# Stationary tiles 576 bytes apart instead of 512 in a two-layer diffusion backbone step

## The reference

```python
def _swiglu(t, wg, wu, wd):
    return (jax.nn.silu(t @ wg) * (t @ wu)) @ wd

def _moe(t, router, wg, wu, wd):
    logits = (t @ router).astype(F32)
    top_v, top_i = lax.top_k(logits, TOP_K)
    gates = jax.nn.softmax(top_v, axis=-1)
    combine = jnp.sum(jax.nn.one_hot(top_i, N_EXPERTS, dtype=F32) * gates[..., None], axis=1)
    out = jnp.zeros_like(t)
    for e in range(N_EXPERTS):
        out = out + combine[:, e:e + 1].astype(t.dtype) * _swiglu(t, wg[e], wu[e], wd[e])
    return out
```

## Time and profile before

| | us |
|---|---|
| median of 3 runs | 1528.2 |
| lowest and highest | 1527.68, 1528.72 |
| the profiled execution | 1526.36 |
| its span, first to last instruction | 1524.5 |

### The profile page before, as it was taken

One profiled execution on the slowest core, in us unless ns is written; L12 is line 12 of the kernel. 1 busy time (PEld: TensorE's weight loads), 2 busy tenths in 40 slices (PEclk: granted clock), 3 DMA queues, 4 the chain that ended last, 5 costly groups with the idle time before them and its releaser, 6 DMA issues.

```text
span 1524.5 us, 21865 instructions
## 1 busy us (share of the span) xinstructions
PE 1471.9 (97%) x7705; PEld 1216.1 (80%) x7705; DVE 1153.6 (76%) x990; ACT 974.4 (64%) x959; POOL 124.9 (8%) x180
## 2 busy tenths in 40 slices
PE   6999999999999989999999999999999999999995
PEld 3867799997777778888888888888888888888884
DVE  2677544445568488888888888888888888888885
ACT  3555633334556467777777777777777777777773
POOL 2521410000030200000000000000000000000001
PEclk9999999999999989999999999999999999999998
DMA  9976975547760889999999999999999999999991
GB/s 351 357 246 214 349 233 190 191 166 259 276 240 1 310 297 382 407 350 407 381 353 399 379 354 391 384 369 382 373 380 367 396 373 359 397 376 345 413 387 48
DMA packets 222629, 489.13 MB, mean 321 GB/s; under 512 B 9040, under 2 KB 42144, under 8 KB 222576
## 3 DMA queue, kind: packets, MB, share of 16 engines
q1 hardware_dynamic: 215024, 466.38, 82.9%
q0 software_dynamic: 7552, 22.03, 4.6%
HBM read 479.53 MB, written 8.85 MB: 320 GB/s over the span
## 4 chain that ended last, share of the span: by engine, by line
PE 92%; DVE 3%; ACT 2%; issue 1%; DMA 1%; POOL 0%; POOLq 0%; SPq 0%; DVEq 0%; ACTq 0%
PE ps L1798 24%; PE ps L1799 24%; PE ps L1803 24%; PE ps L1813 4%; PE ps L1814 3%; PE ps L1820 3%; PE ps L1844 2%; PE ps L2244 2%; PE ps L2023 1%; DMA raw<-in_w_ada 1%; PE ps L1976 1%; PE ps L1998 1%; PE ps L1900 1%; PE ps L1855 1%; PE ps L1867 1%
## 5 line engine op out<-in xcount | busy, mean ns | idle before, releaser
L1243 DVE TENSOR_TENSOR w_lo<-raw,w_hi 128x2048 fp32r<-128x2048 f32 (+1 forms) x397 | 905.4, 2285 | 177.7 <-ACT w_hi L845 177.3
L845 ACT ACTIVATE w_hi<-raw 128x2048 fp32r<-128x2048 f32 (+1 forms) x397 | 757.9, 1914 | 238.7 <-PE ps L1799 216.7
L1798 PE MATMUL ps<-w_hi,x_hi 128*128 128x512 f32 (+1 forms) x1216 | 432.1, 366 | 1.4 <-DVE region L1469 1.4
L1799 PE MATMUL ps<-w_hi,x_lo 128*128 128x512 f32 (+1 forms) x1216 | 426.8, 362 | 0.0
L1803 PE MATMUL ps<-w_lo,x_hi 128*128 128x512 f32 (+1 forms) x1216 | 281.6, 362 | 0.0
L1798 PEld LDWEIGHTS ps<-w_hi,x_hi 128*128 128x128 f32 x1216 | 229.6, 189 | 36.5 <-DVE region L1469 1.6
L1799 PEld LDWEIGHTS ps<-w_hi,x_lo 128*128 128x128 f32 x1216 | 229.7, 189 | 34.0
L1803 PEld LDWEIGHTS ps<-w_lo,x_hi 128*128 128x128 f32 x1216 | 208.0, 189 | 35.5
L1798 PE MATMUL ps<-w_hi,h_hi 128*128 128x512 f32 x520 | 203.3, 391 | 4.9 <-DVE h_lo L1583 4.3
L1799 PE MATMUL ps<-w_hi,h_lo 128*128 128x512 f32 x520 | 202.5, 389 | 0.0
L1803 PE MATMUL ps<-w_lo,h_hi 128*128 128x512 f32 x520 | 137.4, 389 | 0.0
(11 more groups left out here) (271 smaller groups left out, 1081.7 us busy)
## 6 DMA issues: line engine op xcount, KB each, us to landing
raw<-in_moe_w_gate SPq DMA_DIRECT2D x112, 1024.0 KB, 6.7
raw<-in_moe_w_up SPq DMA_DIRECT2D x112, 1024.0 KB, 6.8
raw<-in_moe_w_down SPq DMA_DIRECT2D x112, 1024.0 KB, 7.0
raw<-in_w_ada SPq DMA_DIRECT2D x48, 1024.0 KB, 9.0
raw<-in_w_in SPq DMA_DIRECT2D x20, 960.0 KB, 8.1
raw<-in_ffn_w_gate SPq DMA_DIRECT2D x11, 1024.0 KB, 5.2
raw<-in_ffn_w_up SPq DMA_DIRECT2D x11, 1024.0 KB, 6.3
raw<-in_ffn_w_down SPq DMA_DIRECT2D x11, 1024.0 KB, 5.1
```

The lines of the kernel that those rows point to most:

```text
L845: act.activation(split_hi(c, slice(0, width(c))), raw[:, r % NRAW, 0:width(c)], ACT.Copy).then_inc(hi_done, 1)
L1243: dve.tensor_sub(split_lo(c, n), raw[:, raw_of(c) % NRAW, n], split_hi(c, n)).then_inc(lo_done, 1)
L1798: pe.matmul(out, xh, split_hi(c, w), start=start, stop=False, skip_group_check=True)
L1799: last = pe.matmul(out, xl, split_hi(c, w), start=False, stop=False, skip_group_check=True)
```

## The change

The tile of s and k of x_hi and x_lo now begins `XS` = 144 columns, 576 bytes, after the one before it, and 16 columns stay unused behind each. Both tensors are [128, 2, 8, 144]: 9216 bytes in a partition instead of 8192, so x_lo begins 9216 bytes after x_hi, the tiles of s = 1 4608 bytes after those of s = 0, and all that follows x_lo lies 2048 bytes further on, with the same place modulo 2048. The writers and readers of x take four or eight runs of 128 columns where they took one of 512 or 1024. h_hi and h_lo, the weights and the order of all instructions on all engines are as they were.

```diff
@@ -42,6 +42,7 @@
 NFF = FF // 256
 NJ = FE // 512
 CAP = P
+XS = P + 16
 BLOCK_B = 2048
 
 
@@ -267,9 +268,9 @@
         w_hi3 = nc.alloc_sbuf_tensor_at("w_hi3", [P, UNIT], F32R, offset=qz_at)
         w_lo3 = nc.alloc_sbuf_tensor_at("w_lo3", [P, UNIT], F32R, offset=qz_at + 4 * UNIT)
         x_hi_at = nc.sbuf_base
-        x_hi = sb("x_hi", [P, 2, D], F32R)
+        x_hi = sb("x_hi", [P, 2, KT, XS], F32R)
         probs_all = nc.alloc_sbuf_tensor_at("probs", [P, 2, 2, 4, 256], F32, offset=x_hi_at)
-        x_lo = sb("x_lo", [P, 2, D], F32R)
+        x_lo = sb("x_lo", [P, 2, KT, XS], F32R)
         h_hi = sb("h_hi", [P, 512], F32R)
         h_lo = sb("h_lo", [P, 512], F32R)
         x = sb("x", [P, 2, D])
@@ -349,6 +350,9 @@
 
         def ident(n=P):
             return cst[0:n, C_ID:C_ID + n]
+
+        def o_split(t, s):
+            return t[:, s, :, :].rearrange("p (a k) n -> p a k n", a=2)[:, :, :, 0:P]
 
         def h_of(l, which):
             return hT if which else hTn
@@ -907,7 +911,7 @@
                 q = 4 * l + 2 * which + s
                 for h in halves:
                     act.wait_ge(nh[h], q + 1)
-                    act.activation(x_hi[:, s, 512 * h:512 * h + 512], h_of(l, which)[s][:, 512 * h:512 * h + 512],
+                    act.activation(x_hi[:, s, 4 * h:4 * h + 4, 0:P], h_of(l, which)[s][:, 512 * h:512 * h + 512].rearrange("p (k n) -> p k n", k=4),
                                    ACT.Copy).then_inc(nhi, 1)
 
             def prep(l, s, step):
@@ -1020,7 +1024,7 @@
 
                 for h in range(2):
                     act.wait_ge(m_gath, 2 * n + (h + 1))
-                    act.activation(x_hi[:, 0, 512 * h:512 * h + 512], ps[:, 4 + h, :], ACT.Copy).then_inc(m_xhi, 1)
+                    act.activation(x_hi[:, 0, 4 * h:4 * h + 4, 0:P], ps[:, 4 + h, :].rearrange("p (k n) -> p k n", k=4), ACT.Copy).then_inc(m_xhi, 1)
 
             def moe(p):
                 b = MOE_U + 42 * NE * p
@@ -1183,7 +1187,7 @@
                     rows(0, 4)
                 for s in range(2):
                     act.wait_ge(oT, 2 * l + s + 1)
-                    act.activation(x_hi[:, s, :].rearrange("p (a b) -> p a b", a=2), o_T(s), ACT.Copy).then_inc(o_hi, 1)
+                    act.activation(o_split(x_hi, s), o_T(s).rearrange("p a (k n) -> p a k n", k=4), ACT.Copy).then_inc(o_hi, 1)
                     if l and s == 0:
                         rows(1, 4)
                 post_half(l, 0, 0)
@@ -1310,7 +1314,7 @@
                 for h in halves:
                     n = slice(512 * h, 512 * h + 512)
                     dve.wait_ge(nhi, half_count(q, h))
-                    dve.tensor_sub(x_lo[:, s, n], h_of(l, which)[s][:, n], x_hi[:, s, n]).then_inc(nlo, 1)
+                    dve.tensor_sub(x_lo[:, s, 4 * h:4 * h + 4, 0:P], h_of(l, which)[s][:, n].rearrange("p (k n) -> p k n", k=4), x_hi[:, s, 4 * h:4 * h + 4, 0:P]).then_inc(nlo, 1)
 
             def rope(v, g, w):
 
@@ -1440,8 +1444,7 @@
 
             def out_lo(l, s):
                 dve.wait_ge(o_hi, 2 * l + s + 1)
-                dve.tensor_sub(x_lo[:, s, :].rearrange("p (a b) -> p a b", a=2), o_T(s),
-                               x_hi[:, s, :].rearrange("p (a b) -> p a b", a=2)).then_inc(o_lo, 1)
+                dve.tensor_sub(o_split(x_lo, s), o_T(s).rearrange("p a (k n) -> p a k n", k=4), o_split(x_hi, s)).then_inc(o_lo, 1)
 
             def gated(l, which, s, j=None):
 
@@ -1567,8 +1570,8 @@
             def gathered_lo(n):
                 for h in range(2):
                     dve.wait_ge(m_xhi, 2 * n + (h + 1))
-                    dve.tensor_sub(x_lo[:, 0, 512 * h:512 * h + 512], ps[:, 4 + h, :],
-                                   x_hi[:, 0, 512 * h:512 * h + 512]).then_inc(m_xlo, 1)
+                    dve.tensor_sub(x_lo[:, 0, 4 * h:4 * h + 4, 0:P], ps[:, 4 + h, :].rearrange("p (k n) -> p k n", k=4),
+                                   x_hi[:, 0, 4 * h:4 * h + 4, 0:P]).then_inc(m_xlo, 1)
 
             def moe(p):
                 b = MOE_U + 42 * NE * p
@@ -1823,7 +1826,7 @@
                 return last
 
             def xcols(s, k):
-                return x_hi[:, s, P * k:P * k + P], x_lo[:, s, P * k:P * k + P]
+                return x_hi[:, s, k, 0:P], x_lo[:, s, k, 0:P]
 
             pe.wait_ge(in_cst, 16)
             pe.wait_ge(cond_silu, 1)
```

## The result

| | before | after |
|---|---|---|
| median, us | 1528.46 | 1540.07 |
| lowest and highest | 1527.68, 1529.02 | 1539.15, 1540.65 |
| the profiled execution | 1526.36 | 1540.65 |
| its span | 1524.5 | 1538.8 |

After takes 1.0076 of the time before, with an interval of [1.0058, 1.0093]: 11.6 us slower. The forecast was 1539.

A forecast was written before the change was run, and what follows sets the result against it. The prediction took TensorE, busy 97% of the span, as the bound. It added 8.6 us for 512-column x products and 2.4 for h products, 11.0 in all, giving 1539.2 us; 8-in-10 range 1523 to 1553.

The forecast's parts named there:

- The mechanism: TensorE's weight reads and column reads hinder each other by relative place; a skew changing with k prevents falling into step.
- The signs: Expert x twelves above 2.74 us, repeating k pattern; first seven h steps above 230 ns, later 226.7; dense 120.0; LDWEIGHTS 189.
- Term (1): x products with 512 columns: 2880 matmuls at 3.0 ns more, 8.6 us; ends -8.6 and +17.9 us.
- Term (2): Dense layer's x products with 256 columns, 1056 matmuls: 0, upper end 3.2 us.
- Term (4): h products after x products in 56 expert blocks: seven steps of 6.2 ns each, 2.4 us; lower end 0.
- Term (5): Writes of x_hi and x_lo in runs on ACT and DVE: no cost, at worst 1.6 us.
- Term (3): x products with 480 columns, 480 matmuls already out of step: 0, within 1.4 us either way.
- Place does not matter: Rival: 13.3 ns is a fixed price of changing weights, so 1528.2 us within 1.5; chance 0.33.
- The skew helps: Rival: tiles 64 bytes on make the two reads meet less, -8.6 us, about 1519 us; chance 0.21.

The follow-up runs named there:

- e1: Changed kernel with x tiles 512 bytes apart again, all else of the change kept: 1527.95 us against 1527.71 for the kernel before, ratio 1.0.
- g2: Kernel before with everything from the raw weights' buffers on, moving and stationary tiles alike, 64 bytes later: 1529.22 us, ratio 1.0007.
- e2: Changed kernel with x tiles 512 bytes apart again, but all beginning 64 bytes beyond a multiple of 512: 1540.74 us, ratio 1.0085.
- g3: Changed kernel with x tiles 512 bytes apart again, those of the dense layer alone 64 bytes later: 1522.91 us, ratio 0.997.
- e5: Kernel before with input-projection slices 2048 bytes apart instead of 1920, width still 480 columns: 1527.06 us against 1528.40, ratio 0.9996.
- e4: Changed kernel with x tile k beginning 256 * (k mod 4) bytes after a multiple of 512: 1527.95 us, ratio 0.9998.
- f1: Kernel before with all x tiles 128 bytes later and all h tiles 192 bytes later: 1545.48 us, ratio 1.0115.
- g1: Changed kernel with x tiles 512 bytes apart again, in the dense layer 96 (s = 0) and 192 bytes (s = 1) later: 1525.54 us, ratio 0.998.
- f2: Kernel before with all x tiles 32 bytes later and all h tiles 224 bytes later: 1552.04 us, ratio 1.0159.
- e3: Changed kernel with x tile k beginning 128 * (k mod 4) bytes after a multiple of 512: 1542.08 us, ratio 1.0094.
- f4: Kernel before with all x tiles 16 bytes later and all h tiles 240 bytes later: 1538.12 us, ratio 1.0075.

## Why the prediction was right, and where it was not

**The mechanism** was right in its main point: the time of a step depends on how the stationary tile stands to the moving one. e1 (undoing the place alone removes the loss) and g2 (moving both alike costs nothing) show it. That TensorE's two reads get in each other's way is the reading that fits; no row shows the reads themselves. Its form was wrong: the forecast let a skew that changes with k keep the stream from falling into step, and held that a fixed offset is passed through in any case. e2 shows that a fixed offset costs as much (1540.74 us) and g3 that one can gain. The signs came as listed, but for the 256 columns: twelve x products at 2.77 to 2.78 us (forecast 2.76, bound 2.74); the first seven h steps at 232.9 and the second unit near its old time; the weight load at 188. The single steps of an x unit repeat too: the medians over all units of after are 237, 233, 233, 228, 230, 226, 229, 231 ns for w_hi, and from the fourth step on the same for k 0 to 3 as for k 4 to 7 (the first three depend on what ran before). These two halves agree modulo 256 bytes and not modulo 512, as e4 demands.

**Term (1)**, 2880 x 3.0 = 8.6 us, was 11.9: 4.1 ns each. Its price came from a wrong source. The prediction read the 3 ns of the 480-column stretch as the cost of a skew that changes with k; e5 shows that they stay when the skew is taken away. The irregular single steps were an effect of place, the mean was not, and that the two prices lie near each other (3.0 and 4.1) is luck. The upper end was nearer to what a constant skew costs: 232.9 ns behind the transposes is 6.2 more than 226.7, and 32, 64 or 224 bytes cost 6.6; whether these are the same thing is not shown. The pitch of 576 bytes visits 0, 64, 128 and 192 in turn. By the constant places they cost 0, 6.6 (e2), 5.8 and 2.5 or 6.6 (f1: 2.79 us, and 2.75 or 2.80), on average 3.7 to 4.8 ns by this estimate, beside the 4.1 measured.

**Term (2)**, 0 with an upper end of +3.2, had the wrong sign: -1.9 us. The claim that dense steps stay at 120.0 failed (117.2 and 119.0). No end of that term lay below zero, and it should have: after the changed place was given a price of unknown size for 512 columns, nothing in the rows tied its sign for 256.

**Term (4)**, 2.4 us for h products, measured 2.2, with the seven slow steps as forecast. But a new place does not always bring them: in e2, where x lies at 64 and h at 0, the first h unit takes 2.73 us and not 2.77, and the h products lose 0.4 us on the whole run. **Term (5)**, nothing for runs, is confirmed by 599 and 682 ns, and by e1, which keeps the runs. (Its upper end, half of 32 writes on ACT and 32 on DVE at 0.1 us, would be 3.2 us and not 1.6.) **Term (3)**, 0 within 1.4, was +0.6. The sum of the forecast, 11.0 us, stands beside 12.8 in the steps of the profiled executions and 11.6 between the medians: the error of (1), +3.3, and that of (2), -1.9, have opposite signs. That the total came out better than its parts is luck.

**The rivals.** *Place does not matter* is refuted by after beside e1. It was right on one point that the prediction held against it: the mean of the 480-column stretch stays when the places are put right (e5). *The skew helps* is wrong for 512 columns at every place tried (16 and 240 bytes at best equal place 0), and right for 256, by up to 6.5 ns a step at 64 bytes, which it had not told apart. The Trainium skill, page "SBUF — State Buffer", section "Who interferes with whom", gives TensorE two independent read ports. By the rule that the prediction drew from it, that no place can matter, e2 and g2 would take equal times; they stand at 1.0085 and 1.0007, so the measurement decides against it. The Trainium skill, page "TensorE: Matmul & The Clock Gate", section "Wait — 56ns, not 53.3ns?", gives about 2.5 ns beyond the columns for back-to-back matmuls at 2.4 GHz. Here, with a weight load for each, it is 13.3, between 6.4 (g1, 256 columns at 192 bytes) and 20 by place and length.

Not settled: why the period is 256 bytes, what the 13.3 ns at place 0 are, why 256 columns prefer 64 bytes and 512 prefer 0, and what chooses between the two steps of one place (113.5 and 117.8 with 256 columns, 226.7 and 233.3 at 16 bytes with 512).

## What to carry to other kernels

Where TensorE is the bound and each matmul loads its weights, as in this kernel, the relation of stationary to moving operand modulo 256 bytes is a setting of the kernel: keep both at the same place for 512 columns, try 64 bytes apart for 256 (0.3% here, g3), and judge by starts in the timeline, over many units and not one, and not by durations. A pad or an odd pitch that is put in for another reason can cost 1.6% (f2) with every instruction unchanged. Before a price is taken from another stretch, ask whether it differs from the one at hand in one thing only; the 480-column stretch differed in place and in length.

## What the runs showed of the hardware that was not expected

- The step of a matmul with 512 columns and a weight load: 226.7 ns with the stationary tile at the moving tile's place modulo 256 bytes; on average 233.3 at 32, 64 and 224 bytes beyond and about 232.5 at 128 (f1); either of two at 16 (226.7 or 233.3), at 240 (226.7 or 228.3) and at 192 (229.2 or 233.3).
- With 256 columns: 120.0 ns at place 0; 113.5 or 117.8 at 64 bytes (e2, g3); 113.1 or 117.5 at 192 (g1).
- With 480 columns: 216.3 and 216.7 ns with x tiles at 0, whether slices begin 1920 or 2048 bytes apart; 215.4 (e3) and 218.9 (f4) with x tiles moved.
- The slow return to the step behind transposes (seven steps of 232.9 ns) can also happen between x and h products whose places differ (after, 1022.96 to 1024.59 us: the same 232.9), but need not: in e2 the h unit from 1058.23 to 1060.96 us takes 2.73.
